# Which expert of 32 is loaded into the two spare buffers, and where the tokens' load and first norm and the layer boundary's scalings stand

## The reference, cut to what matters

```python
for l in range(DEPTH):                       # DEPTH = 2
    # adaLN: shift, scale and gate vectors from c (latent) and c_ctx (context)
    mod = jax.nn.silu(c) @ w_mod[l] + b_mod[l]
    h = rms_norm(x, norm1_g[l]) * (1 + sc1) + sh1
    hc = rms_norm(xc, norm1_g[l]) * (1 + csc1) + csh1
    y, yc = token_mixer(h, hc, ...)          # four parallel mixers, merged
    x = x + ga1 * y                          # context too, in layer 0
    tokens = rms_norm(x, norm2_g[l]) * (1 + sc2) + sh2
    f = moe_ffn(tokens, w_router, router_bias, e_gate[l], e_up[l], e_down[l])
    x = x + ga2 * f
return rms_norm(x, final_g)

# moe_ffn: 32 experts, each token goes to 2; per expert
hmid = silu(xb @ e_gate[e]) * (xb @ e_up[e]) # 1024 -> 512, two matrices of 2 MB
y = hmid @ e_down[e]                         # 512 -> 1024, 2 MB
# per token: the two experts' rows, times their weights, are added
```

## Time and profile before

| | |
|---|---|
| median of 3 runs | 2667.63 us (2667.13 to 2670.15) |
| the profiled execution's own time | 2668.15 us |
| its span | 2666.6 us |
| PE busy | 2397.7 us, 90% |
| DVE, ACT, POOL busy | 38%, 19%, 9% |
| mean granted clock of PE | 0.955 |
| moved by DMA | 614.85 MB, mean 231 GB/s |

### The profile page before, as it was taken

The page is one execution under the profiler, slowest core; times in us unless marked ns, Lnnn a source line. Parts: engine busy times, 40 slices in busy tenths (PEclk is TensorE's granted clock), DMA queues, the critical chain, the costliest instruction groups (busy, mean ns, idle before and its releaser), DMA issues.

```text
span 2666.6 us, 45449 instructions
## 1 busy us (share of the span) xinstructions
PE 2397.7 (90%) x19016; PEld 1448.3 (54%) x19017; DVE 1025.3 (38%) x2392; ACT 500.9 (19%) x992; POOL 231.6 (9%) x392
## 2 busy tenths in 40 slices
PE   5999999999999979999999689999999788888874
PEld 2455545454444467777767256567677454444442
DVE  1216545366575333222222332436556522111112
ACT  2023222222231111111101212223222111111111
POOL 3000001000000001111111100000001011111111
PEclk9989999999999979999999898999999889999997
DMA  9111118243344369999999821133466779999994
GB/s 302 63 64 51 46 46 295 111 146 98 109 125 133 146 249 383 408 402 404 390 378 397 306 87 64 63 111 91 166 186 208 272 290 410 414 415 414 413 411 155
DMA packets 151931, 614.85 MB, mean 231 GB/s; under 512 B 16145, under 2 KB 20785, under 8 KB 135249
## 3 DMA queue, kind: packets, MB, share of 16 engines
q1 hardware_dynamic: 126594, 555.91, 54.7%
q0 software_dynamic: 24688, 55.39, 6.6%
q10 hardware_dynamic: 544, 2.10, 0.3%
HBM read 596.39 MB, written 42.11 MB: 239 GB/s over the span
## 4 chain that ended last, share of the span: by engine, by line
PE 66%; DMA 24%; DVE 6%; issue 2%; ACT 1%; POOL 0%; SPq 0%; DVEq 0%; POOLq 0%; ACTq 0%
DMA ring<-in_e_down_dram 23%; PE bank L1459 12%; PE bank L1339 12%; PE bank L1329 7%; PE bank L1723 5%; PE bank L1472 5%; PE score_banks L1740 3%; PE score_banks L1760 3%; PE bank L1630 2%; PE score_banks L1508 2%; PE turned_banks L1518 2%; PE bank L1532 2%; PE bank L1716 2%; PE score_banks L1745 2%; PE bank L1637 1%
## 5 line engine op out<-in xcount | busy, mean ns | idle before, releaser
L1459 PE MATMUL bank<-HT,ring 128*128 128x512 f32 (+1 forms) x1024 | 340.3, 487 | 0.8 <-ACT scr L1029 0.4
L1339 PE MATMUL bank<-ring,HT 128*128 128x512 f32 (+1 forms) x800 | 300.5, 532 | 0.0
L1723 PEld LDWEIGHTS bank<-scr,ring 128*64 128x64 f32 x7936 | 279.0, 138 | 15.5 <-issue 13.9
L1723 PE MATMUL bank<-scr,ring 128*64 128x80 f32 x7936 | 284.4, 234 | 2.2 <-DVE scr L2462 1.0
L1716 PE MATMUL bank<-ring,scr 128*64 128x256 f32 x1984 | 229.2, 384 | 42.7 <-DMA ring<-in_e_gate_dram 21.7
L1459 PEld LDWEIGHTS bank<-HT,ring 128*128 128x128 f32 x1024 | 190.7, 190 | 123.5 <-issue 111.2
L1339 PEld LDWEIGHTS bank<-ring,HT 128*128 128x128 f32 x800 | 151.7, 193 | 135.0 <-issue 128.9
L1716 PEld LDWEIGHTS bank<-ring,scr 128*64 128x64 f32 x1984 | 141.0, 138 | 134.3 <-DMA ring<-in_e_gate_dram 38.1
L1329 PE MATMUL bank<-HT,ring 128*128 128x512 f32 (+1 forms) x512 | 196.0, 541 | 1.9 <-ACT HT L1029 1.9
L1760 PE MATMUL score_banks<-ring,scr 128*64 128x512 f32 x512 | 133.5, 669 | 38.6 <-DMA ring<-in_e_down_dram 37.0
L1329 PEld LDWEIGHTS bank<-HT,ring 128*128 128x128 f32 x512 | 96.9, 192 | 92.0 <-issue 88.5
(11 more groups left out here) (277 smaller groups left out, 2674.8 us busy)
## 6 DMA issues: line engine op xcount, KB each, us to landing
ring<-in_e_down_dram SPq DMA_DIRECT2D x64, 2048.0 KB
ring<-in_e_up_dram SPq DMA_DIRECT2D x62, 2048.0 KB
ring<-in_e_gate_dram SPq DMA_DIRECT2D x62, 2048.0 KB
ring<-in_w_in_dram SPq DMA_DIRECT2D x34, 2048.0 KB
ring<-in_w_mod_dram SPq DMA_DIRECT2D x32, 1024.0 KB, 5.2
...
ys<-consts POOLq DMA_DIRECT2D x1, 10240.0 KB, 36.9
...
```

What stands on the lines that cost most here:

```text
L1339: m = pe.matmul(bank[:, 0:width], HT[:, k, t * P:t * P + P], w[:, k, 0:width], start=k == 0, stop=k == KT_D - 1)
L1459: m = pe.matmul(bank[:, 0:NQ], w[:, k, (ft % 4) * P:(ft % 4) * P + P], HT[:, k, 0:NQ], start=k == 0, stop=k == KT_D - 1)
L1723: m = pe.matmul(ps[bank][rows_, f * cap:f * cap + cap], w[:, k, f * P + hf * HALF:f * P + hf * HALF + HALF], XTv[:, k, :], start=k == 0, s ...
```

## The change

Three things are changed; PE's arithmetic is the same.

1. The two spare buffers hold gate and up of expert 29 (`APART`) in place of expert 1. Expert 1's matrices go into the ring before the first expert starts, and in the loop expert e+2's loads follow on e's from the beginning. Behind the loop experts 30 and 31 take the slots that 27 and 28 leave (`load_hidden(APART - 2, APART + 1, 1)` and the next).
2. In layer 0 the tokens are loaded by SP, behind the fourth `w_mod` block, as eight DMAs of 256 KB (a tile of `x`, a tile of `ctx`, and so on). The norm is done tile by tile: square, mean, root, reciprocal, scaling and shift of one tile before the next, and all of it after the modulation rows.
3. At the layer boundary ACT's four `scale_first` stand between the evacuations of the modulation rows' banks instead of behind all of them.

```diff
 
 CAP = (80, 64)
+APART = EXPERTS - 3
 TILED = (False, True)
...
                     sp.dma_start(dst, src).then_inc(arrived, 16)
+                    if (l, at) == (0, 3):
+                        for t in range(4):
+                            for h, name in enumerate(("x", "ctx")):
+                                sp.dma_start(X[h * HALF:h * HALF + HALF, t, :],
+                                             ins[name][0, t * HALF:t * HALF + HALF, :]).then_inc(x_tile[t], 16)
                     if (l, at) == (0, 0):
                         sp.dma_start(PICK, ins["consts"][:, N_CONST + N_LATE:]).then_inc(pick_loaded, 16)
...
                 sp.wait_ge(mg_done, 32 * (l + 1))
-                load_expert(1, 2, 1)
-                load_expert(2, 1, 1)
+                for c in (1, 2):
+                    load_expert(c, 1, 1)
                 for (s, v), slot in last_users[l]:
                     sp.wait_ge(s, v)
                     load_expert(slot, 0, 0)
                 sp.wait_ge(dense_full, G[l, "h2t", 7] + 1)
+                sp.wait_ge(h2_stored, 64 * (l + 1))
+                load_expert(0, 1, 1)
                 sp.wait_ge(dense_full, G[l, "router", 3] + 1)
-                sp.dma_start(SECOND_GATE, ins["e_gate"][l, 1].rearrange("(p k) n -> p k n", p=P)).then_inc(second_gate_loaded, 16)
-                sp.wait_ge(h2_stored, 64 * (l + 1))
-                load_expert(0, 2, 1)
+                sp.dma_start(APART_GATE, ins["e_gate"][l, APART].rearrange("(p k) n -> p k n", p=P)).then_inc(apart_gate_loaded, 16)
...
@@ -758,7 +766,7 @@
                 eb = l * EXPERTS
                 sp.wait_ge(dense_full, G[l, "rank", 2] + 1)
                 sp.wait_ge(xe_full[0], 8 * eb + 16)
-                sp.dma_start(SECOND_UP, ins["e_up"][l, 1].rearrange("(p k) n -> p k n", p=P)).then_inc(second_up_loaded, 16)
+                sp.dma_start(APART_UP, ins["e_up"][l, APART].rearrange("(p k) n -> p k n", p=P)).then_inc(apart_up_loaded, 16)
...
@@ -772,20 +780,28 @@
                     sp.wait_ge(y_full, 2 * (eb + after + 1))
                     load_expert(2, e, par)
 
-                load_hidden(0, 3, 0)
-                load_down(0, 2, 0)
                 if not TILED[l]:
-                    load_down(1, 3, 1)
-                    with sp.Fori(2, EXPERTS // 2) as i:
+                    with sp.Fori(1, EXPERTS // 2 - 2) as i:
                         for j in range(2):
-                            load_hidden(2 * i + j - 2, 2 * i + j, 1 - j)
+                            load_hidden(2 * i + j - 2, 2 * i + j, j)
                             load_down(2 * i + j - 2, 2 * i + j, j)
+                    load_hidden(APART - 3, APART - 1, 0)
+                    load_down(APART - 3, APART - 1, 0)
+                    load_hidden(APART - 2, APART + 1, 1)
+                    load_down(APART - 2, APART, 1)
+                    load_hidden(APART - 1, APART + 2, 0)
                 else:
-                    with sp.Fori(2, EXPERTS // 2) as i:
+                    load_hidden(0, 2, 0)
+                    with sp.Fori(1, EXPERTS // 2 - 2) as i:
                         for j in range(2):
-                            load_hidden(2 * i + j - 2, 2 * i + j, 1 - j)
-                            load_down(2 * i + j - 3, 2 * i + j - 1, 1 - j)
-                    load_down(EXPERTS - 3, EXPERTS - 1, 1)
+                            load_hidden(2 * i + j - 1, 2 * i + j + 1, 1 - j)
+                            load_down(2 * i + j - 2, 2 * i + j, j)
+                    load_hidden(APART - 2, APART + 1, 1)
+                    load_down(APART - 3, APART - 1, 0)
+                    load_hidden(APART - 1, APART + 2, 0)
+                    load_down(APART - 2, APART, 1)
+                load_down(APART - 1, APART + 1, 0)
+                load_down(APART, APART + 2, 1)
...
 
             act.wait_ge(c_loaded, 32)
             act.activation(csil[:, :, :], craw[:, :, :], ACT.Silu).then_inc(csil_ready, 1)
-            act.dma_start(X[0:HALF, :, :], ins["x"][0].rearrange("(t p) d -> p t d", p=HALF)).then_inc(x_loaded, 16)
-            act.dma_start(X[HALF:P, :, :], ins["ctx"][0].rearrange("(t p) d -> p t d", p=HALF)).then_inc(x_loaded, 16)
-
...
                 PN = rows(l)
                 qt = q_tiles(l)
@@ -1063,31 +1076,32 @@
                 part_evac(1)
                 mod_evac(0)
                 part_evac(2)
+                if l:
+                    scale_first(l - 1, 0)
                 mod_evac(1)
+                part_evac(3)
                 if l:
-                    part_evac(3)
-                    mod_evac(2)
-                    mod_evac(3)
-                    scale_first(l - 1, 0)
                     scale_first(l - 1, 1)
+                mod_evac(2)
+                if l:
+                    scale_first(l - 1, 2)
+                mod_evac(3)
+                if l:
                     square(0)
-                    scale_first(l - 1, 2)
-                    square(1)
                     scale_first(l - 1, 3)
-                    square(2)
-                    square(3)
-                else:
-                    act.wait_ge(x_loaded, 32)
-                    square(0)
                     square(1)
                     square(2)
                     square(3)
-                act.wait_ge(var_ready, l + 1)
-                act.activation(ss[:, :], ss[:, :], ACT.Sqrt).then_inc(std_ready, 1)
-                if l == 0:
-                    part_evac(3)
-                    mod_evac(2)
-                    mod_evac(3)
+                    act.wait_ge(var_ready, l + 1)
+                    act.activation(ss[:, :], ss[:, :], ACT.Sqrt).then_inc(std_ready, 1)
+                else:
+                    for t in range(4):
+                        act.wait_ge(x_tile[t], 32)
+                        square(t)
+                        act.wait_ge(x_var, t + 1)
+                        act.activation(ss[:, t:t + 1], ss[:, t:t + 1], ACT.Sqrt).then_inc(x_std, 1)
+                    act.wait_ge(var_ready, 1)
+                    act.sem_inc(std_ready, 1)
...
                 def hidden_weights(i, j, c):
 
-                    if isinstance(i, int) and (i, j) == (0, 1):
-                        pe.wait_ge((second_gate_loaded, second_up_loaded)[c], 16 * (l + 1))
-                        return (SECOND_GATE, SECOND_UP)[c]
-                    if isinstance(i, int) and (i, j) == (0, 0):
-                        return expert_weights(pe, l, c, 0, 512)
-                    return expert_weights(pe, l, 3 * (1 - j) + c, i - 1 + j, 512)
+                    e = 2 * i + j if isinstance(i, int) else 0
+                    if e == APART:
+                        pe.wait_ge((apart_gate_loaded, apart_up_loaded)[c], 16 * (l + 1))
+                        return (APART_GATE, APART_UP)[c]
+                    if e == APART + 1:
+                        return expert_weights(pe, l, 3 + c, EXPERTS // 2 - 2, 512)
+                    if e == APART + 2:
+                        return expert_weights(pe, l, c, EXPERTS // 2 - 1, 512)
+                    return expert_weights(pe, l, 3 * j + c, i, 512)
...
@@ -1927,18 +1944,38 @@
                 mod_arrived(1)
                 step(dve.scalar_tensor_tensor(out=MODA[:, D:2 * D], in0=MODA[:, D:2 * D], scalar=1.0, in1=G1,
                                               op0=ALU.add, op1=ALU.mult))
-                dve.wait_ge(ss_ready, 4 * (l + 1))
-                dve.tensor_scalar(ss[:, :], ss[:, :], 1.0 / D, EPS, ALU.mult, ALU.add).then_inc(var_ready, 1)
-                dve.wait_ge(std_ready, l + 1)
-                step(dve.reciprocal(rstd[:, :], ss[:, :]))
-                for t in range(4):
-                    last = dve.scalar_tensor_tensor(out=HTOK[:, t, :], in0=X[:, t, :], scalar=rstd[:, t:t + 1],
+                def add_shift(t):
+
+                    dve.tensor_tensor(HTOK[:, t, :], HTOK[:, t, :], MODA[:, 0:D], ALU.add).then_inc(h_ready, 1)
+
+                def add_scale(t):
+
+                    return dve.scalar_tensor_tensor(out=HTOK[:, t, :], in0=X[:, t, :], scalar=rstd[:, t:t + 1],
                                                     in1=MODA[:, D:2 * D], op0=ALU.mult, op1=ALU.mult)
-                step(last)
-                mod_arrived(2)
-                mod_arrived(3)
-                for t in range(4):
-                    dve.tensor_tensor(HTOK[:, t, :], HTOK[:, t, :], MODA[:, 0:D], ALU.add).then_inc(h_ready, 1)
+
+                if l == 0:
+                    mod_arrived(2)
+                    mod_arrived(3)
+                    for t in range(4):
+                        dve.wait_ge(ss_ready, t + 1)
+                        dve.tensor_scalar(ss[:, t:t + 1], ss[:, t:t + 1], 1.0 / D, EPS, ALU.mult, ALU.add).then_inc(x_var, 1)
+                        dve.wait_ge(x_std, t + 1)
+                        step(dve.reciprocal(rstd[:, t:t + 1], ss[:, t:t + 1]))
+                        step(add_scale(t))
+                        add_shift(t)
+                    dve.sem_inc(var_ready, 1)
```

(12 more changed lines are left out.)

24 lines of the change are left out of this document (13 added, 11 removed).

## The result

The changed kernel takes 2653.14 us (median of 5 runs, 2652.34 to 2656.36) against 2667.42 (5 runs, 2667.13 to 2670.15): the ratio is 0.9936, with a 95 % interval from 0.9924 to 0.9947. The forecast was 2657.2, 4 us more, and the range of 2650 to 2664 holds the result. The profiled execution is the slowest of the five: 2656.36 us, span 2654.7, 11.9 us shorter than the span of before.

What follows compares the result with a forecast made beforehand. The chain that ended last went through PE in the dense parts and loads of `e_down` in the experts. −3.2 + 1.8 − 7.6 − 1.4 = −10.4: 2657.7 against the profiled execution, 2657.2 against the median; range 2650 to 2664.

Steps and rivals of the forecast that it cites:

- The start, -3.2: From program start to first projection: modulation blocks come sooner, projection at 55.4 against 58.86; 3.2 us less, bounds −5 and +1.6.
- the old 3.6 us from the last shift to the first projection: At the start: the kernel before's distance, kept unchanged, puts the first projection at 55.4 after four tiles end at 51.8.
- The experts of layer 0, +1.8: Layer 0's experts: at most 0.4 us saved at down 31, later loads 2.2 us later; 1.8 us more, bounds −1 and +4.
- the push: Expert loads delayed by bytes that don't fit the idle stretch: 2.2 us in layer 0, 5.0 in layer 1.
- The boundary, -7.6: Between the layers: first scaling starts at 1508.3 instead of 1515.95; 7.6 us less, bounds −11 and −5.5.
- its own sign of being wrong: Layer boundary, down 31 to DVE's last output: a gain under 5 or over 9 us would show the prediction wrong.
- the rival of the pause: PE's 5.46 us pause before the next layer's modulation waits for its block; shrinking by 3 gives 2654; chance 0.15.
- Layer 1, -1.4: Layer 1's experts: 6.4 us gained at the last experts, 5.0 lost to later loads; 1.4 us less, bounds −5 and +4.
- The tail: Layer 1's last experts: without later loads, down 31 ends at 2630.2 against 2636.6, 6.4 us less.
- the stream's end: Both expert stages: the end of the load stream decides, not queue places; 8.5 and 5.7 us gained, 2642.6; chance 0.07.
- the tokens were not late: Start: late token loads would give 2662, or 2667 with small DMAs one after the other; chance 0.14 together.
- the idle stretches could be filled: Expert stages: rival that they can't, all 10.7 us delaying loads in both layers, 2671.4 or 2674.6; chance 0.04.

Runs made afterwards that it cites:

- Turns_between: The changed kernel with ACT evacuating a tile's turned tokens behind the next tile's root, not all eight behind the fourth root: 2656.66 us, ratio 0.9935.
- the second: Profile of the changed kernel run once more, unaltered: 2655.31 us, ratio 0.9930.
- the old order of downs: The changed kernel's load order; a follow-up kernel instead loaded layer 1's downs 28 and 29 ahead of gate and up of 30 and 31: 2650.48 us.

## Why the prediction was right, and where it was off

**The start, -3.2.** The terms up to the last shift held within 0.4 us: last part 30.63 (30.2), ACT free 37.30 (36.9), four tiles done 51.94 (51.8), pitch 3.07 (3.16), one table load. The term that failed is "the old 3.6 us from the last shift to the first projection". It measured 4.96, because three banks fill up and ACT empties none until its fourth root; I had named that and allowed it 0.3 us (3.46 less 3.2), where it cost 1.3. Turns_between bears this out: with the evacuations moved, the distance is 2.9. So -2.0 at the first projection. And the sum carried this number to the end of the program without asking what lies between: in the first profile the clock took it all and 1.7 us more (207.72 before, 209.44 now), in the second it gave 2 us on top (203.69).

**The experts of layer 0, +1.8.** The first profile says +2.9. Over ten profiles with the experts' part the stage took 505.4 to 510.0 us, mean 507.3; over four without, 505.0 to 507.9, mean 506.5. The effect is about +0.8 and lies within what single executions differ by. Within the bounds. Whether it is the push that I had reckoned is not shown: from down 0 to down 12 the six profiles with the old order of downs are 2 us ahead of the four without the part (means 186.8 and 188.8), and at the end stand PE's new pauses, which the sum did not have.

**The boundary, -7.6.** The scalings alone give -7.0: the mechanism and its place were right. Together with the experts' part it is -10.9 at the first projection, at the edge of the bounds (-11), and -11.7 at DVE's last output, where the prediction said to measure: over its own sign of being wrong, "less than 5 or more than 9 us". This is where the result left the forecast. The failed step is that the sum kept PE's pause and the modulation's first parts as they were. With the experts' part the pause is 2.4 us shorter (3.04 for 5.46), and the products of parts 0 and 1 take 5.6 us from the first to the last instead of 7.8. I gave the rival of the pause 0.15, with "a branch over the overflow code lies there too" as the argument against it; but if the pause is a load of instructions that waits behind the stream, the branch is no argument against it. The packets and shares above fit that reading; the other one, PE's experts written out, is not excluded. So that rival's time (2654) is nearly the measured one, and the cause of the shorter pause stays open. The gathers did hold the scalings, by 0.68, 0.76 and 0.89 us, less than the 1.1 that I had at worst; with the modulation sooner, the first of them is what ACT waits for.

**Layer 1, -1.4.** The first profile gives -2.95; the mean of six profiles with this part (and the old order of downs) is 486.8 us, of four without 487.4. So -0.6 or so, inside the scatter. But its two terms nearly cancel, and each of them shows in all of these profiles; both were sized too large. The tail: from down 29 to down 31 18.2 us instead of 23.3, so -5.1 for my -6.4, with no wait for gate and up of 29 to 31, as forecast; over the same six and four profiles it is 16.5 to 19.5 us against 21.4 to 23.3, means -4.5. The push: measured from expert 0's gate (2135.89 against 2144.61), down 28 starts 1.6 us later than before and down 29 2.2 us, where I had 5.0; over the six and four, down 29 stands 467.1 to 471.6 us behind that gate against 464.3 to 467.1, means +4.0.

**The sum.** -10.4 against -11.8 of the profiled execution and -14.3 between the medians. From the two profiles the -11.7 at layer 1's down 31 is made up so: up to down 0 of layer 0 +0.2, layer 0's experts +2.9, the boundary -10.9, layer 1's dense part -0.9, its experts -2.95. Beside -3.2, +1.8, -7.6, nothing and -1.4 that is 3.4 us too much at the start and 3.3 too little at the boundary, which cancel: that the sum is so near is in part luck. The mechanisms of the scalings and of the tail held; the start's term held at its own place (-2.0 for -3.2) and was then taken by the clock, which no term of mine had. Of the other rivals, the stream's end did not decide (it wanted 8.5 and 5.7 us from the two expert stages), the tokens were not late (tile 0's square starts at 37.30 with no wait for its rows, and the tiles follow at 3.07), and the idle stretches could be filled: 1.00 in place of 0.08.

The Trainium skill's rule to batch calls by table set (ScalarE: Activation LUTs, "Table sets: the hidden batching unit") cost nothing here: square and root alternate over four tiles, and ACT shows a single table load, 1.28 us. By the fixed 2 us per transfer that the Trainium skill states (SBUF — State Buffer, "The DMA setup-cost knee"), with the 26 us and the 8 us from tile 3's landing to the first projection of the prediction, the first projection would stand at about 65 us, an estimate, and not at 56.90. In the trace the eight transfers of 256 KB show no such pause: from 30 to 38 us the DMA engines are full, at 240 GB/s (POOL's small loads are in this), and no square waits for its rows.
